# Closing LayerNorm: the last chunk's small sums ahead of half of the chunk in front, in another PSUM bank; layer 1's coefficients behind the additions

## What is computed

```python
for i in range(2):
    hp, hs = x * (1 + sc1) + sh1                  # modulation
    o = mixer_i(h)                                # i = 0 long convolution, i = 1 attention
    x = layer_norm(ALPHA * x + g1 * o, ln1_g[i], ln1_b[i])
    f = swiglu(x * (1 + sc2) + sh2)               # 1024 -> 2 x 2816 -> 1024
    x = layer_norm(ALPHA * x + g2 * f, ln2_g[i], ln2_b[i])
```

## Time and profile before

| | us |
|---|---|
| median of 3 runs | 3808.89 (3808.26 to 3813.37) |
| the profiled execution, its whole time | 3808.96 |
| its span in the trace | 3807.1 |
| TensorE busy | 3598.1 (95%) |
| VectorE busy | 1515.6 (40%) |
| GpSimd busy | 1230.0 (32%) |
| ScalarE busy | 1033.6 (27%) |
| mean granted TensorE clock, share of full speed | 0.979 |

### The profile page before, as it was taken

The page is one execution under the profiler, slowest core; times in us unless marked ns, Lnnn a source line. Parts: engine busy times, 40 slices in busy tenths (PEclk is TensorE's granted clock), DMA queues, the critical chain, the costliest instruction groups (busy, mean ns, idle before and its releaser), DMA issues. The chain is left out here.

```text
span 3807.1 us, 47310 instructions
## 1 busy us (share of the span) xinstructions
PE 3598.1 (95%) x19244; PEld 3065.7 (81%) x19244; DVE 1515.6 (40%) x2472; ACT 1033.6 (27%) x1554; POOL 1230.0 (32%) x815
## 2 busy tenths in 40 slices
PE   8999998898899999999989998999899999999997
PEld 6788887677788888888868877888778888888885
DVE  2765553454524444434451014777341122111116
ACT  1441111132421111111152224777433111111113
POOL 1531113623532222222361213666343222222223
PEclk9999999999999999999999999999999999999998
DMA  3253323754122122221234355777201111111111
GB/s 118 87 168 117 105 90 134 247 187 145 49 72 67 61 78 72 76 68 62 77 120 161 144 174 158 179 178 171 84 28 39 35 39 39 39 38 35 39 39 61
DMA packets 178710, 369.58 MB, mean 97 GB/s; under 512 B 17063, under 2 KB 102567, under 8 KB 176840
## 3 DMA queue, kind: packets, MB, share of 16 engines
q1 hardware_dynamic: 173064, 356.21, 29.7%
q10 hardware_dynamic: 5440, 10.49, 0.9%
HBM read 286.93 MB, written 79.69 MB: 96 GB/s over the span
## 5 line engine op out<-in xcount | busy, mean ns | idle before, releaser
L148 POOL TENSOR_TENSOR w_lo<-w_raw,w_hi 128x1024 fp32r<-128x1024 f32 x210 | 506.0, 2410 | 1509.1 <-ACT w_hi L142 1509.1
L156 PE MATMUL ps_r<-a_hi,w_hi 128*128 128x512 f32 (+1 forms) x2496 | 640.4, 358 | 17.1 <-POOL a_lo L1716 11.4
L156 PE MATMUL ps_r<-a_hi,w_lo 128*128 128x512 f32 (+1 forms) x2496 | 635.8, 356 | 0.0
L156 PE MATMUL ps_r<-a_lo,w_hi 128*128 128x512 f32 (+1 forms) x2496 | 635.6, 356 | 0.0
L142 ACT ACTIVATE w_hi<-w_raw 128x1024 fp32r<-128x1024 f32 (+1 forms) x217 | 225.3, 1038 | 1018.3 <-PE ps_r L156 563.4
L156 PEld LDWEIGHTS ps_r<-a_hi,w_hi 128*128 128x128 f32 x2496 | 415.2, 188 | 100.3 <-POOL a_lo L1716 19.2
L156 PEld LDWEIGHTS ps_r<-a_lo,w_hi 128*128 128x128 f32 x2496 | 415.1, 188 | 74.0 <-issue 1.5
L156 PEld LDWEIGHTS ps_r<-a_hi,w_lo 128*128 128x128 f32 x2496 | 415.1, 188 | 73.6
L1909 DVE TENSOR_TENSOR hid_l<-hid_l,ps_r 128x1280 f32<-128x1280 f32 x44 | 65.5, 1488 | 840.7 <-PE ps_r L156 840.7
L1929 DVE SCALAR_TENSOR_TENSOR x_t_l<-ps_r,mod,x_t_l 128x1024 f32<-128x1024 f32 (+1 forms) x288 | 241.4, 880 | 264.6 <-PE ps_r L156 264.6
L1756 POOL TENSOR_TENSOR hid_lo_l<-hid_l,hid_hi_l 128x1280 fp32r<-128x1280 f32 x42 | 134.4, 3201 | 488.1 <-ACT hid_hi_l L1657 488.1
(11 more groups left out here) (227 smaller groups left out, 6038.2 us busy)
## 6 DMA issues: line engine op xcount, KB each, us to landing
w_raw<-in_w_all SPq DMA_DIRECT2D x213, 512.0 KB, 3.6
ada_w_l<-in_ada_t SPq DMA_DIRECT2D x59, 512.0 KB, 3.5
v_hl<-v_d SPq DMA_DIRECT2D x128, 128.0 KB, 2.9
t_tail_f<-in_ada_t SPq DMA_DIRECT2D x24, 512.0 KB, 4.2
spec<-gout_f SPq DMA_DIRECT2D x80, 128.0 KB, 2.1
g_spec_c<-spec ACTq DMA_DIRECT2D x20, 512.0 KB, 5.7
y_d<-y_spec_c SPq DMA_DIRECT2D x40, 256.0 KB, 3.5
v_d<-z_v_l SPq DMA_DIRECT2D x10, 1024.0 KB, 4.6
```

The costliest lines, as they stand in the source:

```text
L148: pool.tensor_tensor(wl[:, s, 0:width], raw[:, s, 0:width], wh[:, s, 0:width].bitcast(F32), ALU.subtract).then_inc(w_split, 1)
L156: last = pe.matmul(out[:, c0:c1], w[:, c % 2, blk * 128:blk * 128 + 128], x[:, c0:c1], start=start and b == 0 and term == 0, stop=stop and ...
```

## The change

1. The last chunk's small products of the closing LayerNorm are written to `pg[1]` instead of `px` (columns 512 on, in the squares' first buffer), they have a semaphore of their own, `stat_e`, for which `variance` waits, and TensorE's wait for the normalised chunk in front stands behind them, ahead of the wide product.
2. Of the second chunk, tiles 4 to 7 are no longer normalised after m = 6 and 7 of the last chunk, but behind its last `add_square`. ScalarE does tiles 4 and 5 ahead of the last chunk's root and 6 and 7 behind it. GpSimd (layer 0) does tiles 4 to 7 behind the last `add_x` and ahead of two weight splits, which keep their place ahead of the last chunk's tiles.
3. In layer 1 `modulation` stands behind the additions of m = 0 to 5 instead of at the start.

```diff
--- before.py
+++ after.py
@@ -1303,7 +1303,7 @@
                 xs_ok, coef1, coef2, xa_ok, y_out = [sem(n, st) for n in ("xs_ok", "coef1", "coef2", "xa_ok", "y_out")]
                 silu, gated, hh_ok, hl_ok, out_mm, out_ok = [
                     sem(n, st) for n in ("silu", "gated", "hh_ok", "hl_ok", "out_mm", "out_ok")]
-                hl_e = sem("hl_e", st)
+                hl_e, stat_e = sem("hl_e", st), sem("stat_e", st)
                 cb_in, cb_ok, aw_in, ad_ok, aw_in2, ad_ok2, md_ok, md_r = [
                     sem(n, st) for n in ("cb_in", "cb_ok", "aw_in", "ad_ok", "aw_in2", "ad_ok2", "md_ok", "md_r")]
                 aw_in = [aw_in, sem("aw_in1", st)]
@@ -1429,13 +1429,18 @@
                         done = adds(ln, pos(ln, 7, ci)) + 1
                         pe.wait_ge(ln.s1_ok, done)
                         pe.wait_ge(ln.s2_ok, done)
-                        if ci:
+                        last = ln is n2 and ci == 2
+                        if ci and not last:
                             pe.wait_ge(ln.xn, 8 * ci)
+                        small = pg[1] if last else px
                         for v, s in enumerate((s1, s2)):
                             for n in range(tiles):
                                 o = 512 + 2 * (v * tiles + n)
-                                pe.matmul(px[:, o:o + 2], s[:, c0 + 128 * n:c0 + 128 * n + 128], meanw[:, 0:2],
-                                          start=True, stop=True)
+                                ins = pe.matmul(small[:, o:o + 2], s[:, c0 + 128 * n:c0 + 128 * n + 128], meanw[:, 0:2],
+                                                start=True, stop=True)
+                        if last:
+                            ins.then_inc(stat_e, 1)
+                            pe.wait_ge(ln.xn, 8 * ci)
                         pe.matmul(px[:, 0:c1 - c0], meanw[:, :], s1[:, c0:c1], start=True, stop=True).then_inc(ln.stat, 1)
 
                     def spread(ln, ci):
@@ -1673,6 +1678,12 @@
                                 split_hi(act, e + 2 + j, r, 12)
                     rounds(step_in, step_out)
 
+                    def end_part(ci, ks):
+                        if last_layer:
+                            final(ci, ks)
+                        else:
+                            modulate(n2, ci, ks)
+
                     for ci in range(3):
                         for m in range(8):
                             square(n2, m, ci)
@@ -1682,16 +1693,13 @@
                                 root(n2, ci - 1)
                             if ci == 1 and m == 3 and not last_layer:
                                 act.wait_ge(coef2, 5)
-                            if ci and m >= 4:
-                                if last_layer:
-                                    final(ci - 1, range(2 * m - 8, 2 * m - 6))
-                                else:
-                                    modulate(n2, ci - 1, range(2 * m - 8, 2 * m - 6))
+                            if ci == 1 and m >= 4 or ci == 2 and m in (4, 5):
+                                end_part(ci - 1, range(2 * m - 8, 2 * m - 6))
+                    end_part(1, range(4, 6))
                     root(n2, 2)
-                    if last_layer:
-                        final(2, range(8))
-                    else:
-                        modulate(n2, 2, range(8))
+                    end_part(1, range(6, 8))
+                    end_part(2, range(8))
+                    if not last_layer:
                         qkv_act(act)
 
                 @block.gpsimd
@@ -1766,9 +1774,10 @@
                     for ci in range(3):
                         for m in range(8):
                             add_x(n2, m, ci)
-                            if ci and m >= 4 and not last_layer:
+                            if not last_layer and (ci == 1 and m >= 4 or ci == 2 and m in (4, 5)):
                                 low(n2, ci - 1, range(2 * m - 8, 2 * m - 6))
                     if not last_layer:
+                        low(n2, 1, range(4, 8))
                         split_lo(pool, eq)
                         split_lo(pool, eq + 1)
                     if not last_layer:
@@ -1802,8 +1811,12 @@
 
                     def variance(ln, ci):
                         w = width(ln, ci) // 64
-                        dve.wait_ge(ln.stat, ci + 1)
-                        dve.tensor_copy(cm[:, 0:2 * w], px[:, 512:512 + 2 * w]).then_inc(ln.cst, 1)
+                        if ln is n2 and ci == 2:
+                            dve.wait_ge(stat_e, 1)
+                        else:
+                            dve.wait_ge(ln.stat, ci + 1)
+                        small = pg[1] if ln is n2 and ci == 2 else px
+                        dve.tensor_copy(cm[:, 0:2 * w], small[:, 512:512 + 2 * w]).then_inc(ln.cst, 1)
                         dve.wait_ge(ln.cst, 4 * ci + 1)
                         dve.tensor_tensor(cv[:, 0:w], cm[:, 0:w], cm[:, 0:w], ALU.mult).then_inc(ln.cst, 1)
                         dve.wait_ge(ln.cst, 4 * ci + 2)
@@ -1847,9 +1860,8 @@
                                                      op0=ALU.mult, op1=ALU.add,
                                                      accum_out=acc_a[:, n, q:q + 1]).then_inc(done, 1)
 
-                    if layer == 1:
-                        dve.wait_ge(xs_ok, KT)
-                    modulation(dve, coef1, layer, SC2, SH2, 4 * layer)
+                    if layer == 0:
+                        modulation(dve, coef1, layer, SC2, SH2, 4 * layer)
                     for m in range(6):
                         for ci in range(3):
                             if ci == 0:
@@ -1863,6 +1875,8 @@
                                 dve.wait_ge(aw_in[n % 2], 16 * (n // 2) + 16)
                                 ada_row(n, (aw, aw2)[n % 2], cb0, ad_ok)
                     dve.wait_ge(xs_ok, KT)
+                    if layer == 1:
+                        modulation(dve, coef1, layer, SC2, SH2, 4 * layer)
                     if layer == 0:
                         dve.wait_ge(ad_ok, 16)
                         dve.tensor_tensor(mod[:, 40:48, :], acc_a[:, 0:8, :],
@@ -1944,9 +1958,11 @@
                                 variance(n2, ci - 1)
                             if ci and m == 2:
                                 inverse(n2, ci - 1)
-                            if ci and m >= 4:
+                            if ci == 1 and m >= 4 or ci == 2 and m in (4, 5):
                                 normalise(n2, ci - 1, 2 * m - 8)
                         add_square(n2, 7, ci)
+                    normalise(n2, 1, 4)
+                    normalise(n2, 1, 6)
                     variance(n2, 2)
                     inverse(n2, 2)
                     for k in range(0, KT, 2):
```

## The result

| | us |
|---|---|
| before, median of 4 runs | 3808.73 (3808.26 to 3813.37) |
| changed, median of 4 runs | 3788.49 (3784.91 to 3792.16) |
| ratio | 0.9944, 95% interval 0.9927 to 0.9961 |
| profiled execution of the changed kernel, whole and span | 3788.51, 3786.7 |
| mean granted clock | 0.981 (before 0.979) |

The change gives 20.2 us, by the interval 15 to 28; 19.65 were predicted, and 3789.2 us. The page's first part stands as in the earlier trace rows: the same work, and less time in which TensorE stands still or runs slowly.

The account below looks back on a forecast made before the run. TensorE, busy 95% of the span, bounds the kernel, so only its stops and half-clock stretches can give time. From 3808.89 us, -9.95 + 1.1 - 5.0 - 5.8 = -19.65 gives 3789.2 us, range 3784.5 to 3797.

Parts of the forecast that it names:

- Layer 1's start: First products of layer 1: TensorE's 7.85 us stop goes, and 2.1 us at the lower clock with it: -9.95 us.
- the rival that another wait holds the fifth group: Layer 1's start: another wait (square, weights, bank) holds TensorE's fifth group, so nothing is gained there; 3799.2 us, chance 4%.
- The coefficients: Layer 1's first chunk: one of five moved instructions waits 1.3 us for GpSimd, TensorE stands 1.1 us: +1.1 us.
- Layer 1's end: Layer 1's closing normalisation: put-off tiles hide the small products, last chunk's first multiplication comes earlier: -5.0 us.
- Layer 0's end: Layer 0's closing normalisation to the third q/k/v product: earlier multiplication, cached keys and product, clock kept: -5.8 us.
- the term of the third product: Layer 0's end: third q/k/v product starts 4.2 us earlier, and 1.6 us of lost clock behind its stop go.
- Not 4 us or more earlier: Sign of being wrong, layer 0's end: the third q/k/v product does not come 4 us or more earlier.
- Rival (1): Layer 0's end: ScalarE and GpSimd become the bound, DMA keeps its old times, gain 0 there; 3795.0 us, chance 13%.
- The slower rival (4): Layer 0's end: clock stays low through two q/k/v weights, costing 28 us; 3817 us, chance 2%.
- rival (3): Later stops move by several us; one or two now free cost 1.6 us each in clock; 3792 us, chance 9%.
- The sum: Whole kernel: the four terms total -19.65 us from the median 3808.89, giving 3789.2 us.

Follow-up runs that it names:

- layer 1's end alone: Kernel before with only layer 1's closing normalisation in the new order and bank, all else as before: 3801.2 us (11 runs), ratio 0.9978.
- the coefficients alone: Kernel before with only layer 1's coefficient instructions moved behind the additions of m = 0 to 5: 3797.9 us (5 runs), ratio 0.9965.
- changed again: The changed kernel itself, unedited, run once more beside the kernel before on another chip: 3788.79 us (7 runs), ratio 0.9948.
- layer 0's end alone: Kernel before with only layer 0's closing normalisation in the new order and bank: 3801.92 us (11 runs), ratio 0.9981.
- bank alone: Changed kernel with the other bank and early semaphore, but the old order of tiles 4 to 7; coefficients stay moved: 3798.92 us (one execution).
- order alone: Changed kernel with the late order of tiles 4 to 7, but without the other bank and early semaphore; coefficients stay moved: 3801.21 us (one execution).
- the last attempt: Changed kernel with coefficients inside m = 5, layer 0's GpSimd splits and low parts reordered around a wait, first cached-key loads earlier: 3789.69 us (7 runs), ratio 0.9958.

## Why the prediction was right, point by point

**Layer 1's start: right.** The row of 7.85 us is gone and nothing took its place; the rival that another wait holds the fifth group fell. Predicted -9.95; six traces with the move (without the one profiled first) have 81.87 to 82.14, mean 81.99, and three without it 91.80 to 92.47, mean 92.06: -10.1. With the one profiled first, 83.35, it is -9.9. The profiled pair alone shows -8.45, and 1.1 us of the difference is the longer time at low clock behind its first scaling.

**The coefficients: right, mechanism and size.** Predicted +1.1 with one of five instructions held for 1.3 us; measured +1.03, one held for 1.14. The rule of the Trainium skill that the prediction weighed (page "SBUF — State Buffer", section "Who interferes with whom") agrees with this and with the blocked pairs above, and so do the starts: the first of the five, 0.17 us, began at 2782.52, 0.03 us ahead of GpSimd's third addition, the second behind it.

**Layer 1's end: right.** Predicted -5.0, measured -4.91. I had the small products at half clock to 3784.2; in the changed kernel they ran at full, 1.02 us for eight, and with layer 1's end alone at half, 1.84, behind the same stop of 2.32 us. The distance is 18.95 and 18.94: hidden behind VectorE's tiles they cost nothing at either level. The wide product and the spread ran at half, as assumed.

**Layer 0's end: the term of the third product was a little too large.** Predicted -4.2 and 1.6 of clock. Measured: the multiplication 5.75 earlier (predicted 6.0), the cached key 3.69 (4.2), the third product 3.87 (4.2), and 1.7 of clock, the stop having shrunk to 1.42 us. GpSimd ran its eight `low` in 10.63 us, where I had 8 times 1.28, or 10.2. "Not 4 us or more earlier" stood among the prediction's signs of being wrong, and by distance this term misses it by 0.13 us; the 6.6 us between the two absolute times hold 2.7 of the head. Rival (1), that GpSimd and ScalarE at the end of the queue give all of it back, fell; what it gives back is the difference of 5.75 and 3.87. The slower rival (4) fell too. After the stop from 1957.7 to 1961.3 TensorE was back at its full clock by about 1965, in the changed kernel's windows:

```profile
1960.00:1965.00 5.00, 3.71 (x17) 3.74 (x18) 5.00 (x10) 2.31 (x5) 5.00 (x4) 0.50 0.60 229
1965.00:1970.00 5.00, 5.00 (x27) 4.22 (x26) 1.23 (x3) 5.00 (x8) 4.84 (x4) 0.97 0.73 235
```

Is the clock's 1.7 us kept? In part, as far as the traces tell. At the end of TensorE's next long stop (2205.82 before), counted from the first 512-column normalisation, the three kernels with layer 0's end as before (the kernel before, the coefficients alone, layer 1's end alone) have 265.90, 266.26 and 266.28 us, the three with it changed and nothing added (changed, changed again, layer 0's end alone) 261.05, 261.33 and 261.23. That is -4.9, not -5.6. The bank alone lies there at 265.86 and the order alone at 262.60, 3.5 us sooner than before, though its third product was 0.5 later; TensorE's idle time and its clock behind that product don't account for it, it is one execution, and the cause stays open.

**The clock at later stops, rival (3): its mechanism is real, its price is not, and it isn't of the change's making.** Behind the stop of 2.60 us, where the clock stayed full before, it fell in the changed kernel. Two windows of the changed kernel and one of the changed again, then TensorE 5.3 us behind that stop, before and changed:

```profile
3700.00:3705.00 5.00, 2.39 (x13) 2.19 (x12) 2.02 (x2) 1.20 (x2) 5.00 (x3) 0.76 0.34 105
3705.00:3710.00 5.00, 4.95 (x37) 4.74 (x37) 2.96 (x8) 2.34 (x6) 4.07 (x5) 0.89 0.01 3
...
3705.00:3710.00 5.00, 5.00 (x30) 4.83 (x29) 2.51 (x6) 2.37 (x5) 4.17 (x4) 0.68 0.01 3
...
3723.70 0.38 PE L1538 MATMUL ps_r<-hid_hi_l,a_hi 128*128 128x256 f32 x1 [1.41 <-POOL a_lo L1752]
...
3708.16 0.39 PE L1543 MATMUL ps_r<-hid_hi_l,a_hi 128*128 128x256 f32 x1
```

1.6 and 1.7 us of TensorE's time, the price I had put at 1.6. The kernels with the coefficients alone and with layer 1's end alone show it as well, and the other six of the ten traces don't, though the stop is the same and five of these kernels carry parts of the change. And it costs nothing: at full clock TensorE stands once more, 1.41 to 1.61 us in the six, until GpSimd's split of a weight is done; at the lower clock it comes to the same product later and hardly waits (5.25 us behind the first stop before, 5.27 changed). From the first stop's end to the first 512-column normalisation all ten take 52.1 to 52.3 us. That the whole stretch from small products to closing normalisation is 967.92 in both profiled kernels has the same two sides: by the traces the changed kernel loses 4.7 us there at the lower clock, before it was 1.7, and stands still for 11.2 us, before 13.4.

**The sum.** By distances that repeat: -3.9 - 1.7 - 10.1 + 1.0 - 4.9 = -19.6, as forecast, or -18.9 if layer 0 is counted to the next long stop. That the median came out within 0.6 us of the forecast is luck: the second time the medians gave 18.9 (3807.72 to 3788.79), unchanged stretches alone move a run by several us, and the last seven runs of the changed kernel reach from 3772.91 to 3793.02.

## What to carry to other kernels

Where an engine both finishes old work and is needed for a short chain of new results, put the old work over the other engine's part of that chain, and check first that the two don't share a buffer: up to the first multiplication the order alone was worth -1.2 and +0.8 us, the bank alone -0.2 and -2.1, both together -5.7 and -4.9. Tiny VectorE instructions on the path are not cheap where GpSimd streams: in a quiet place five cost 0.8 us, beside it two cost 3.6 instead of 0.34. Before a gap is closed further, ask whether TensorE will only stand longer at the next one: in the last attempt the clock behind that stop took back 2.6 of 2.8 us. And before lost clock is counted as lost time, look whether TensorE would have stood right behind anyway.

## What the runs showed of the hardware that I had not expected

- GpSimd held VectorE once per instruction of its own, not once in all: 1.35 then 2.26 us end with the first and the second split, 0.93 then 2.27 with a `low` and a split. The instruction count of the small chain decides as much as its place. Which of the two had started first told too: the same coefficient instruction (`tensor_scalar`, 16 columns) took 0.17 us when it began just ahead of GpSimd's addition (2782.52 against 2782.55), and 1.00 us when it began 0.32 us behind one (2770.00 against 2769.68).
- Behind the same stop of TensorE of 2.60 us the clock fell in four executions and not in six, and the time up to the next normalisation was the same (52.1 to 52.3 us). At the third q/k/v product, by contrast, the length told in all ten: behind stops of 1.31 to 1.50 us (four traces) no TensorE time was lost, behind those of 3.32 to 3.95 (five) 1.5 to 1.7 us each, behind that of 4.75 2.6 us.
- Stretches of the same program vary more than most of the local edits give: the head takes 1935.5 to 1940.0 us, third product to layer 1's scaling 699.4 to 704.9, layer 1's feed-forward part 963.2 to 971.3. In this feed-forward part the time lost at the lower clock (1.7 to 8.3 us) and TensorE's idle time (11.2 to 13.4) account for most of it: without both, nine of the ten traces leave 951.9 to 952.9 us. The tenth, layer 1's end alone, leaves 947.8, and why isn't shown.
